# A streaming encoder layer: the gate's norm folded behind its mix, operand splits moved into the passes, and a fourth accumulator copy per pair

## The chip, the cores and the metric

The kernel runs on one NeuronCore of a Trainium2 chip. The metric is device time in microseconds for one execution; before the change three runs took 1078.3, 1076.97 and 1076.26 us, so the median is 1076.97 us. The execution under the profiler took 1074.96 us, with a span of 1073.2 us from its first to its last instruction.

The engines are called by the profile's names: PE is TensorE, which multiplies (PEld is its weight load), DVE is VectorE, ACT is ScalarE, POOL is GpSimd, and SP only issues transfers. Each engine runs its own list of instructions strictly in order, and semaphores are the only link between the lists.

## The reference

One layer is computed for 2048 prompt frames and 8 x 16 sample frames, with d = 1024.

```python
h = x @ w_in                                   # 3 * 512 columns for part A, 4 * 512 for part B
u_a = gelu(h[..., 0:512])
v_a = layernorm(gelu(h[..., 512:1024]), ln_v_g, ln_v_b)
z_a, q, k, v_b, z_b = the five groups of 512 columns that follow
# part A, in chunks of 128 frames, 4 groups g of 128 channels c
mix = einsum('gts,bnsgc->bntgc', tril(w_s), v_a) + b_s      # b_s: one number per g and t
a_out = u_a * mix
# part B: attention over the own 64-frame chunk and the 8 before it, 8 heads, relative bias
b_out = softmax(q k^T / 8 + bias) v_b
y = concat(a_out * silu(z_a), b_out * silu(z_b))
out = layernorm(ALPHA * x + y @ w_out, ln_g, ln_b)
```

The sample frames take the same path with cached keys and values; k, v_b and the normalised v_a of the sample frames are outputs too (`gv_out` holds the last).

## The kernel before

The 2176 frames are 17 token tiles of 128. All matrix products are done on rounded operands (fp32r) in three parts: every operand is split into a high part, which ACT makes by a copy, and a low part, which DVE makes by subtracting the high part from the original. PE then adds high x high, high x low and low x high.

**The va stage** (17 tiles, some 130 us). For tile t PE does `project_tile("va", t, ..)` in two halves h (L1667, 12 products of 512 columns each), and between the halves `mix(t - 2)` (L1683, four plain fp32 products of 128 columns). ACT moves the projection out of PSUM with Gelu (L1131), DVE does the layer norm on it in four instructions (L1412 statistics, L1414 their mean and variance, L1416 subtract and times gain, L1425 times rstd and plus offset), with rstd from POOL (L957, L959). ACT copies the mix out (L1061), POOL adds b_s (L939), and SP stores it to the scratch tensor `s_mix`. Beside that, the tiles' own operands `xt_f`, `xt_h`, `xt_l` are loaded and split two tiles ahead (L1047 on ACT, L1340 on DVE), and the operand of the first pass is prepared.

**The two passes** (some 200 and 227 us) compute everything but va and v_b, for 1024 and 1152 frames. A pass has ten pairs m of 128-column blocks, in the order u, za, u, za, k, k, q, q, z, z. A pair is 2 x 2 blocks, computed with seven products p = 0..6 in place of eight. The seven right operands are combinations of x: `xo_h[a][p]`, `xo_l[a][p]`, each in four pieces kc; POOL forms the combinations (`sum_x`, L905), ACT and DVE split the 28 pieces of a pass (L1054, L1346). The seven left operands `wf` are built one pair ahead (POOL L923 to L929, ACT L1042, DVE L1334). The table `X_IN_TILE` says in which tile, and `X_IN_STEP` in which product of the pass, a piece is split; 24 pieces are split in the va stage and 4 in products 0 to 3 of the first pass, and all 28 of the second pass in the eight v tiles between the passes.

Products accumulate in four PSUM tiles: p = 0, 2, 4 in `sums[0]`, p = 3 in `sums[1]`, p = 1 and 6 in `sums[2]` (the names pt_ps in the profile), p = 5 in `sums[3]`. ACT copies `sums[0]` after p = 0, 2 and 4 (`copy_sum`, L1071). DVE forms the four results ("units") of a pair by one addition each (`add_sums`, L1360), after p = 3, 4, 5 and 6. The second addition reads `sums[2]`, which p = 6 writes on top of, so p = 6 waits for it (`pe.wait_ge(added, 4 * m + 2)`). The first product on `sums[2]` of the next pair (p = 1) waits for all four additions.

A u unit gets Gelu on ACT (L1078) and is multiplied with its part of the mix on POOL (`gate_u`, L949); the part comes back from `s_mix` by a transfer into one of two buffers `mixb`, and the transfer of unit j + 2 waits for gate j. Other units get a Tanh or copy on ACT and one or two operations on DVE (`finish_unit`).

**Token tiles of v_b**: eight between the passes, five behind the second pass, four more beside the first attention steps; the rest of the run (from 667 us) is attention and the output projection. Between the passes the second pass's x is loaded (`load_xo(1, ..)`), summed on POOL (16 instructions) and split. In these stretches tile t + 1's operand shares its memory with the accumulator copies, so SP loads it after the last addition of the pass.

The order of work is written out by hand: each engine's list is what its loops and tables say. What stands behind a waiting instruction waits with it, SP's transfers too.

## Time and profile before

| | PE | DVE | ACT | POOL |
|---|---|---|---|---|
| busy, us (share of the span of 1073.2) | 1010.8 (94%) | 716.9 (67%) | 515.6 (48%) | 324.6 (30%) |
| instructions | 7456 | 1230 | 1018 | 269 |

| | us |
|---|---|
| median of three runs | 1076.97 |
| profiled execution, its own time | 1074.96 |
| its span | 1073.2 |

The profiled execution lies 2.0 us under the median. The busy figure of PE hides three things: matmul records overlap in the pipeline, a product at the half clock counts as busy for twice as long, and 94% is a mean over stages. So the stages are read one by one: the granted clock and the busy time of each stretch, then the gaps of PE on the timeline with the engine that ended each of them, then what that engine's own list did in the gap.

### The profile page before, as it was taken

What the parts mean: (1) busy time and instruction counts of PE and PEld (TensorE: products, weight loads), DVE (VectorE), ACT (ScalarE), POOL (GpSimd) and SP (SyncE); (2) the same over time, 40 slices, a digit from 0 to 9 for tenths busy, and PEclk for the clock granted to TensorE, in tenths of its full rate; (3) what the DMA queues carried; (4) which work ended last, traced back from release to release, by engine and by line L of the source; (5) the groups of instructions that cost most, each with busy time, mean ns of one, the idle gap of its engine ahead of it and who ended that gap; (6) DMA issues with size and microseconds to landing.
All of it is one profiled execution on the core that took longest, in us unless ns stands there. A gap on an engine that the chain in (4) does not pass through costs nothing.

```text
span 1073.2 us, 19266 instructions
## 1 busy us (share of the span) xinstructions
PE 1010.8 (94%) x7456; PEld 865.3 (81%) x7456; DVE 716.9 (67%) x1230; ACT 515.6 (48%) x1018; POOL 324.6 (30%) x269
## 2 busy tenths in 40 slices
PE   7979889999998789999999989999999999999997
PEld 6867677878886569999999977777888888888885
DVE  5959976476565794646555551596777777786765
ACT  5335443334444453333434342575666666666630
POOL 2635753532330834242322200003322222223201
PEclk9998999999999889999999999999999999999999
DMA  6684333346456723323455466575344433433222
GB/s 237 190 232 157 99 108 105 114 121 175 148 145 210 247 94 98 89 92 94 146 175 152 128 200 229 199 261 206 131 149 139 157 133 131 157 121 109 90 80 79
DMA packets 126363, 158.95 MB, mean 148 GB/s; under 512 B 13608, under 2 KB 76224, under 8 KB 126272
## 3 DMA queue, kind: packets, MB, share of 16 engines
q1 hardware_dynamic: 111296, 130.45, 37.8%
q10 hardware_dynamic: 14976, 27.27, 8.0%
q8 instruction: 59, 0.97, 0.4%
q14 instruction: 32, 0.26, 0.1%
HBM read 112.57 MB, written 48.26 MB: 150 GB/s over the span
## 4 chain that ended last, share of the span: by engine, by line
PE 72%; DVE 13%; DMA 6%; issue 3%; ACT 2%; SPq 2%; POOL 1%; ACTq 0%; DVEq 0%
PE s_ps L1713 19%; PE oo_ps L1894 15%; PE pt_ps L1713 9%; PE s_ps L1667 6%; PE oo_ps L1856 6%; PE s_ps L1785 5%; DVE xo_l L1346 4%; PE oo_ps L1713 4%; DMA xt_f<-x_tiles 3%; PE pt_ps L1827 3%; DVE wf L1334 2%; DVE cs L1360 2%; PE s_ps L1894 2%; DVE xt_l L1340 1%; ACT st L1085 1%
## 5 line engine op out<-in xcount | busy, mean ns | idle before, releaser
L1713 PE MATMUL s_ps<-xo_h,wf 128*128 128x288 f32 (+1 forms) x960 | 233.7, 328 | 4.2 <-DVE wf L1334 4.2
L1667 PE MATMUL s_ps<-wp,xt_h 128*128 128x512 f32 x448 | 148.8, 415 | 32.5 <-DVE xt_l L1340 32.0
L1713 PEld LDWEIGHTS s_ps<-xo_h,wf 128*128 128x128 f32 x960 | 164.2, 188 | 17.6 <-DVE xo_l L1346 4.6
L1713 PE MATMUL s_ps<-xo_l,wf 128*128 128x288 f32 (+1 forms) x480 | 157.0, 327 | 0.0
L1667 PEld LDWEIGHTS s_ps<-wp,xt_h 128*128 128x128 f32 x448 | 87.1, 200 | 55.2 <-issue 30.7
L1713 PE MATMUL pt_ps<-xo_h,wf 128*128 128x288 f32 (+1 forms) x480 | 120.8, 329 | 6.8 <-DVE cs L1360 6.6
L1492 DVE CUSTOM_DVE_ANT_1 prob<-s_ps,bias 128x640 f32<-128x640 f32 (+1 forms) x112 | 85.7, 803 | 59.0 <-PE s_ps L1785 59.0
L1228 ACT ACTIVATE prob<-prob,low 128x640 f32<-128x640 f32 (+3 forms) x128 | 97.4, 762 | 45.5 <-DVE low L1492 45.4
L1894 PE MATMUL oo_ps<-wo_h,yh 128*128 128x512 f32 x248 | 100.5, 405 | 0.0
L1334 DVE TENSOR_TENSOR wf<-s,wf 128x512 fp32r<-128x512 f32 x60 | 51.6, 862 | 69.6 <-ACT wf L1042 69.6
L1894 PE MATMUL oo_ps<-wo_h,yl 128*128 128x512 f32 x248 | 97.0, 391 | 0.0
L1894 PE MATMUL oo_ps<-wo_l,yh 128*128 128x512 f32 x248 | 97.0, 391 | 0.0
L1713 PEld LDWEIGHTS pt_ps<-xo_h,wf 128*128 128x128 f32 x480 | 82.3, 188 | 17.2 <-DVE wf L1334 9.0
L1713 PEld LDWEIGHTS s_ps<-xo_l,wf 128*128 128x128 f32 x480 | 90.5, 188 | 6.3
L923 POOL TENSOR_TENSOR s<-a,a 128x512 f32<-128x512 f32 x20 | 26.5, 1323 | 220.3 <-DMA a<-w_pair 220.3
L1667 PE MATMUL s_ps<-wp,xt_l 128*128 128x512 f32 x224 | 91.2, 407 | 0.0
L1334 DVE TENSOR_TENSOR wf<-a,wf 128x512 fp32r<-128x512 f32 x80 | 76.1, 964 | 19.4 <-ACT wf L1042 19.4
L1340 DVE TENSOR_TENSOR xt_l<-xt_f,xt_h 128x512 fp32r<-128x512 f32 x68 | 56.1, 837 | 47.6 <-ACT xt_h L1047 47.6
L1516 DVE TENSOR_SCALAR prob<-prob,rden 128x640 f32<-128x640 f32 (+4 forms) x128 | 79.5, 621 | 4.6
L1713 PE MATMUL pt_ps<-xo_l,wf 128*128 128x288 f32 (+1 forms) x240 | 78.2, 326 | 0.0
L1071 ACT ACTIVATE copy<-s_ps 128x512 f32<-128x512 f32 (+1 forms) x60 | 37.2, 620 | 83.3 <-PE s_ps L1713 83.3
L1002 POOL TENSOR_TENSOR rstd_o<-mv_o,eps 128x1 f32<-128x1 f32 x17 | 3.2, 190 | 235.9 <-DVE mv_o L1567 206.3
(154 smaller groups left out, 2069.1 us busy)
## 6 DMA issues: line engine op xcount, KB each, us to landing
a<-w_pair ACTq DMA_DIRECT2D x80, 256.0 KB, 2.7
...
```

The source lines that it names most:

```text
L1071: nc.scalar.activation(wide(copies[p // 2], pas), sum_at(p, pas), ACT.Copy).then_inc(copied, 1)
L1228: nc.scalar.activation(prob[s][:, 0:n], prob[s][:, 0:n], ACT.Exp, bias=low[:, s:s + 1], scale=-1.0, accum_out=den[:, s:s + 1]).then_inc(ex ...
L1334: nc.vector.tensor_tensor(wf[:, p, 1], operand[p][:], wf[:, p, 0].bitcast(f32), ALU.subtract).then_inc(w_ready, 1)
L1340: nc.vector.tensor_tensor(xt_l[b][h][:], xt_f[b][h][:], xt_h[b][h][:].bitcast(f32), ALU.subtract).then_inc(xt_ready, 1)
L1346: nc.vector.tensor_tensor(xo_l[a][p][:, kc, :], xo_f[a][p][:, kc, :], xo_h[a][p][:, kc, :].bitcast(f32), ALU.subtract).then_inc(xo_ready, 1)
L1492: nc.vector.tensor_tensor_reduce(out=out, in0=src, in1=b, scale=1.0, scalar=MASKED, op0=ALU.add, op1=ALU.min, accum_out=low[:, s:s + 1]).t ...
L1516: nc.vector.tensor_scalar(prob[s][:, lo:n], prob[s][:, lo:n], rden[:, s:s + 1], None, ALU.mult).then_inc(normed, 1)
L1667: made = nc.tensor.matmul(out, xx[b][h][:, kc % HK, :], wp[:, kc, side, :], start=(h, i, a) == (0, 0, 0), stop=(h, i, a) == (1, HK - 1, 2))
L1713: made = nc.tensor.matmul(out, wf[:, p, side, kc, :], xx[pas][p][:, kc, c * n:(c + 1) * n], start=kc == 0 and a == 0 and p in (0, 1, 3, 5) ...
L1785: last = nc.tensor.matmul(s_ps[h][:, at_c:at_c + count * P], q[t % 2][rows, a * GRP + p, :], key_slots(rows, c * GRP + p, first, count), s ...
L1856: last = nc.tensor.matmul(o_ps[64 * h:64 * h + 64, p * P:(p + 1) * P], v[(t + 1 - nk + b) % KR][:, p * P + 64 * h:p * P + 64 * h + 64], pt ...
L1894: last = nc.tensor.matmul(out_bank(half), y[n % 2][:, c, :], w[h][:, c, :], start=c == 0 and a == 0, stop=c == KC - 1 and a == 2)
```

## The change

Three things are changed.

**The norm.** With v = n * g + b, where n is the normalised tile without gain and offset, the mix is W v = g * (W n) + b * rowsum(W). So DVE's two instructions per tile (gain and offset) go; ACT normalises in place by one instruction (`normalise_va`, scale rstd, bias `shift_v` = -mean * rstd, which POOL makes by one more small instruction). PE computes the row sums once, by two fp32 products of 512 columns in front of mix(0), into the PSUM tiles `row_ps`, the first of which is also the output of mix(1). DVE turns them into `mix_b` and `mix_bs` by 4 + 4 instructions of 128 x 128 at the end of its tile 2, and mix(1) waits for the first four. POOL's 17 additions of b_s go, and DVE's eight copies that filled `bss`; gain and offset come back in `scale_mix`, one DVE instruction per u unit (two in the second pass) on the reloaded `mixb`, ahead of that unit's `add_sums`. `gv_out` is made by two DVE instructions in the first pass.

**The splits.** Of the 28 pieces of a pass, the 16 of p = 0..3 are split in the token tiles (tiles 3 to 14 of va; tiles 2, 3, 5, 6 of v), and the 12 of p = 4..6 in products 0 to 3 of the pass, three each. The loads of x move from tiles 0, 2, 5, 8 to 0, 1, 3, 5, and POOL does two sums per tile in tiles 1 to 8. The operand halves have seven places instead of three pairs: half 0 of the second v tile of a stretch goes to the memory of `mixb`, and is loaded in the last pair of the pass; half 1 is loaded one addition earlier and ahead of the last unit's store. The reloads of v tiles 0 and 1 for attention move behind the load of v tile 12.

**The fourth copy.** Ahead of the copy after p = 4, ACT also copies `sums[2]` to `copies[0]`. The second addition then reads two copies, and p = 6 waits for that ACT copy instead of for the addition. In every product the weight builds now stand ahead of `hand` and `finish_unit`.

```diff
-COPY_OF = [0, 2, 2, 1]
+COPY_OF = [0, 0, 2, 1]
...
+X_FIRST = [(kc, p) for kc in range(HK) for p in range(4)]
+X_REST = [(kc, p) for p in range(4, OPS) for kc in range(HK)]
...
-X_IN_TILE[0].setdefault(16, []).extend([(3, 0), (3, 1), (3, 2)])
-for _j in range(28):
-    X_IN_TILE[1].setdefault(min(1 + _j // 4, V_MID - 1), []).append((_j // 7, _j % 7))
-X_IN_STEP = [{0: [(3, 3)], 1: [(3, 4)], 2: [(3, 5)], 3: [(3, 6)]}, {}]
...
+for _j, _piece in enumerate(X_FIRST):
+    X_IN_TILE[0].setdefault(3 + 3 * _j // 4, []).append(_piece)
+    X_IN_TILE[1].setdefault((2, 3, 5, 6)[_j // 4], []).append(_piece)
+X_IN_STEP = {step: X_REST[3 * step:3 * step + 3] for step in range(4)}
...
+    if kind == "v" and h == 0 and t in (1, V_MID + 1):
+        return 6
+    if tile_seq(kind, t) % 2:
+        return 2 + h
+    return 4 + h if kind == "v" and t > V_MID else h
...
-        copies = [at(f"copy{j}", copy_at + 4 * WIDTH[1] * j, [WIDTH[1]]) for j in range(3)]
+        copies = [at(f"copy{j}", copy_at + 4 * WIDTH[1] * i, [WIDTH[1]]) for j, i in enumerate((1, 0, 2))]
...
+        mix_b, mix_bs = at("mix_b", here, [GRP, P]), at("mix_bs", here + 2048, [GRP, P])
...
+        row_ps = [out_ps, pt_both[:, 1].rearrange("p g t -> p (g t)")]
...
-                    if h == 0 and t in (0, 2, 5, 8):
-                        load_xo(0, (0, 2, 5, 8).index(t))
+                    if h == 0 and t in (0, 1, 3, 5):
+                        load_xo(0, (0, 1, 3, 5).index(t))
...
+                            load_xt("v", t + 1, 0)
+                sp.wait_ge(added, 4 * NP * (pas + 1) - 1)
+                load_xt("v", V_MID * pas + 1, 1)
...
-            sp.wait_ge(u_mixed, len(U_UNITS))
...
+                if t == V_MID + 2:
+                    sp.wait_ge(xt_freed, tile_number("v", V_MID + 1))
+                    load_v(0)
+                    load_v(1)
...
-            def add_bias_s(t):
...
-                pool.wait_ge(mixb_loaded[j % 2], 16 * (j // 2 + 1))
+                pool.wait_ge(mix_scaled, j + 1)
...
-                if t >= 1:
-                    sum_x(0, t - 1)
-                if t >= 2:
-                    add_bias_s(t - 2)
+                for j in (2 * t - 2, 2 * t - 1):
+                    if 0 <= j < 16:
+                        sum_x(0, j)
...
+                pool.wait_ge(rstd_v_ready, t + 1)
+                nc.gpsimd.tensor_scalar(shift_v[:], mv_v[:, 0:1], rstd_v[:], -1.0,
+                                        ALU.mult, ALU.mult).then_inc(shift_v_ready, 1)
...
+            def normalise_va(t):
+                act.wait_ge(shift_v_ready, t + 1)
+                nc.scalar.activation(st[t % 2][:, 0:512], st[t % 2][:, 0:512], ACT.Identity, bias=shift_v[:],
+                                     scale=rstd_v[:]).then_inc(vn_ready, 1)
...
+                if p == 4:
+                    act.wait_ge(added, 4 * m + 1)
+                    nc.scalar.activation(wide(copies[0], pas), sum_at(1, pas), ACT.Copy).then_inc(copied, 1)
...
-                    act.wait_ge(added, 4 * m - 3 if p == 0 else 4 * m)
-                pas = m // NP
+                    act.wait_ge(added, 4 * m - 2 if p == 0 else 4 * m)
...
-                dve.wait_ge(copied, 3 * m + (1 if p == 3 else 3))
-                nc.vector.tensor_tensor(wide(unit_sum(n), pas), sum_at(p, pas) if p != 4 else sum_at(1, pas),
+                dve.wait_ge(copied, 4 * m + (1 if p == 3 else 4))
+                nc.vector.tensor_tensor(wide(unit_sum(n), pas), sum_at(p, pas) if p != 4 else wide(copies[2], pas),
...
+            def scale_mix(n):
+                if n not in U_COUNT:
+                    return
+                pas, _, g, tb = unit_of(n)
+                j = U_COUNT[n] - 1
+                dve.wait_ge(mix_b_ready, 2 * GRP)
+                dve.wait_ge(mixb_loaded[j % 2], 16 * (j // 2 + 1))
+                held, add = mixb[j % 2][:, 0:512].rearrange("p (n t) -> p n t", t=P), mix_b[:, g, :]
+                made = nc.vector.scalar_tensor_tensor(out=held, in0=held, scalar=v_cols[:, g:g + 1],
+                                                      in1=bass.AP(add.tensor, add.offset, [add.ap[0], [0, 4], [1, P]]),
+                                                      op0=ALU.mult, op1=ALU.add)
+                if pas:
...
-                nc.vector.scalar_tensor_tensor(out=va, in0=va, scalar=mv_v[:, 0:1], in1=lnvg[:], op0=ALU.subtract,
-                                               op1=ALU.mult).then_inc(vn_centred, 1)
...
-                nc.vector.scalar_tensor_tensor(out=va, in0=va, scalar=rstd_v[:], in1=lnvb[:], op0=ALU.mult,
-                                               op1=ALU.add).then_inc(vn_ready, 1)
...
+                if t == 2:
+                    dve.wait_ge(cols_loaded, 32)
+                    dve.wait_ge(row_sums, 2)
+                    for g in range(GRP):
+                        nc.vector.scalar_tensor_tensor(out=mix_b[:, g, :], in0=row_ps[0][:, g * P:(g + 1) * P],
+                                                       scalar=v_cols[:, GRP + g:GRP + g + 1], in1=bs[:, g, :],
+                                                       op0=ALU.mult, op1=ALU.add).then_inc(mix_b_ready, 1)
...
+                    for what in step_builds(step):
+                        w_low_part(what)
+                    for kc, o in X_IN_STEP.get(step - first, ()):
+                        xo_low_part(pas, kc, o)
                     if p >= 4:
                         finish_unit(4 * m + p - 4)
                     if p == 0 and step > first:
                         finish_unit(4 * m - 1)
-                    for what in step_builds(step):
-                        w_low_part(what)
...
+                    if p >= 3:
+                        scale_mix(4 * m + p - 3)
...
+                    for row, held in zip(row_ps, (wt, wts)):
+                        nc.tensor.matmul(row[:], st[3][:, 0:P], held[:].rearrange("p g t -> p (g t)"),
+                                         start=True, stop=True).then_inc(row_sums, 1)
...
+                if t == 1:
+                    pe.wait_ge(mix_b_ready, GRP)
...
-                    pe.wait_ge(added, 4 * m + 2)
+                    pe.wait_ge(copied, 4 * m + 3)
```

How the lists move, at three places. First DVE in va tile 9, before (xt_l and xo_l are the low parts, st the tile):

```order
L1412 BN_STATS stats_v_148<-st1_115 128x6
L1414 BN_AGGR mv_v_149<-stats_v_148 128x2
L1416 SCALAR_TENSOR_TENSOR st1_115<-st1_115,mv_v_149,lnvg_91 128x512
L1340 TENSOR_TENSOR xt_l1_0_132<-xt_f1_0_138,xt_h1_0_126 128x512
L1346 TENSOR_TENSOR xo_l0_1_64<-xo_f0_1_78,xo_h0_1_50 128x512
L1346 TENSOR_TENSOR xo_l0_2_65<-xo_f0_2_79,xo_h0_2_51 128x512
L1425 SCALAR_TENSOR_TENSOR st1_115<-st1_115,rstd_v_150,lnvb_92 128x512
L1340 TENSOR_TENSOR xt_l1_1_133<-xt_f1_1_139,xt_h1_1_127 128x512
```

and the same tile after:

```order
L1445 BN_STATS stats_v_152<-st1_114 128x6
L1449 BN_AGGR mv_v_153<-stats_v_152 128x2
L1358 TENSOR_TENSOR xt_l2_132<-xt_f2_139,xt_h2_125 128x512
L1364 TENSOR_TENSOR xo_l0_0_63<-xo_f0_0_77,xo_h0_0_49 128x512
L1364 TENSOR_TENSOR xo_l0_1_64<-xo_f0_1_78,xo_h0_1_50 128x512
L1358 TENSOR_TENSOR xt_l3_133<-xt_f3_140,xt_h3_126 128x512
```

The two scaled instructions on st are gone; this tile still has two pieces of xo, others have one.

Second, DVE in va tile 2, before:

```order
L1412 BN_STATS stats_v_148<-st0_114 128x6
L1414 BN_AGGR mv_v_149<-stats_v_148 128x2
L1416 SCALAR_TENSOR_TENSOR st0_114<-st0_114,mv_v_149,lnvg_91 128x512
L1340 TENSOR_TENSOR xt_l0_0_130<-xt_f0_0_136,xt_h0_0_124 128x512
L1425 SCALAR_TENSOR_TENSOR st0_114<-st0_114,rstd_v_150,lnvb_92 128x512
L1340 TENSOR_TENSOR xt_l0_1_131<-xt_f0_1_137,xt_h0_1_125 128x512
```

and after (mix_b is what mix(1) on PE waits for):

```order
L1445 BN_STATS stats_v_152<-st0_113 128x6
L1449 BN_AGGR mv_v_153<-stats_v_152 128x2
L1358 TENSOR_TENSOR xt_l0_130<-xt_f0_137,xt_h0_123 128x512
L1358 TENSOR_TENSOR xt_l1_131<-xt_f1_138,xt_h1_124 128x512
L1460 SCALAR_TENSOR_TENSOR mix_b_146<-oo_ps,v_cols_157,bs_93 128x128 x4
L1465 SCALAR_TENSOR_TENSOR mix_bs_147<-pt_ps,v_cols_157,bs_93 128x128 x4
```

The first four of the new instructions stand behind both halves' splits of tile 4.

Third, DVE from the first addition of pair 0 (u) on, before:

```order
L1360 TENSOR_TENSOR u0_0_110<-s_ps1,copy0_97 128x512
L1334 TENSOR_TENSOR wf_101<-a11_106,wf_101 128x512
L1360 TENSOR_TENSOR u1_1_113<-pt_ps,copy2_99 128x512
L1334 TENSOR_TENSOR wf_101<-s1_100,wf_101 128x512
L1360 TENSOR_TENSOR u1_0_112<-oo_ps,copy2_99 128x512
L1334 TENSOR_TENSOR wf_101<-s2_109,wf_101 128x512
L1360 TENSOR_TENSOR u0_1_111<-pt_ps,copy1_98 128x512
```

and after (mixb is a reloaded part of the mix, cs and u are results, copy the accumulator copies):

```order
L1429 SCALAR_TENSOR_TENSOR mixb0_117<-mixb0_117,v_cols_157,mix_b_146 128x512
L1380 TENSOR_TENSOR u0_0_109<-s_ps1,copy0_96 128x512
L1352 TENSOR_TENSOR wf_100<-a11_105,wf_100 128x512
L1429 SCALAR_TENSOR_TENSOR mixb1_118<-mixb1_118,v_cols_157,mix_b_146 128x512
L1380 TENSOR_TENSOR u1_1_112<-copy2_98,copy0_96 128x512
L1352 TENSOR_TENSOR wf_100<-s1_99,wf_100 128x512
L1429 SCALAR_TENSOR_TENSOR mixb0_117<-mixb0_117,v_cols_157,mix_b_146 128x512
L1380 TENSOR_TENSOR u1_0_111<-oo_ps,copy2_98 128x512
L1352 TENSOR_TENSOR wf_100<-s2_108,wf_100 128x512
L1429 SCALAR_TENSOR_TENSOR mixb1_118<-mixb1_118,v_cols_157,mix_b_146 128x512
L1380 TENSOR_TENSOR u0_1_110<-pt_ps,copy1_97 128x512
```

Each addition to u now stands behind an instruction that needs a transfer into mixb, and the second addition reads two copies.

## Rows read from the trace of the kernel before

**Rows 1.** Stretches: us, busy (instructions) by engine, PEclk, DMA share, GB/s.

```profile
22.63:73.69 51.06, 51.06 (x256) 43.10 (x256) 43.49 (x52) 18.80 (x34) 27.81 (x29) 1.00 0.62 183
73.69:137.98 64.29, 48.14 (x225) 38.97 (x225) 58.36 (x66) 31.48 (x57) 38.97 (x36) 0.92 0.48 149
137.98:337.56 199.58, 196.00 (x856) 159.89 (x857) 125.64 (x160) 81.73 (x145) 71.89 (x49) 0.99 0.47 138
337.56:404.05 66.49, 50.89 (x194) 39.47 (x192) 52.20 (x52) 32.97 (x59) 32.90 (x19) 0.87 0.52 170
404.05:631.08 227.03, 223.85 (x1682) 222.84 (x1682) 124.73 (x153) 87.71 (x160) 65.46 (x45) 1.00 0.42 124
631.08:666.97 35.89, 30.55 (x122) 23.95 (x121) 10.88 (x17) 10.50 (x18) 1.50 (x4) 0.90 0.71 246
```

**Rows 2.** Chain that ended last, in time: start, us, piece, instructions merged.

```profile
241.31 2.72 PE s_ps L1713 x12
...
244.03 2.98 PE pt_ps L1713 x12
...
420.18 3.18 PE oo_ps L1713 x24
```

**Rows 3.** Timeline, PE, 80 to 140: start, us, line, operation, idle before.

```profile
81.53 1.19 PE L1667 MATMUL s_ps<-wp,xt_h 128*128 128x512 f32 x2 [7.84 <-DVE xt_l L1340]
...
121.95 1.16 PE L1683 MATMUL oo_ps<-wt,st 128*128 128x128 f32 x8 [1.29 <-DVE st L1425]
...
129.87 1.16 PE L1683 MATMUL oo_ps<-wt,st 128*128 128x128 f32 x8 [1.28 <-DVE st L1425]
...
137.98 0.76 PE L1713 MATMUL s_ps<-xo_h,wf 128*128 128x512 f32 x1 [4.18 <-DVE wf L1334]
```

**Rows 4.** Timeline, PE, 170 to 180: product 6 of a pair.

```profile
177.72 0.47 PE L1713 MATMUL pt_ps<-xo_h,wf 128*128 128x512 f32 x1 [0.88 <-DVE cs L1360]
```

**Rows 5.** Timeline, PE then POOL, 340 to 400: token tiles between the passes.

```profile
377.87 1.19 PE L1667 MATMUL s_ps<-wp,xt_h 128*128 128x512 f32 x2 [4.09 <-DVE xt_l L1340]
...
351.59 29.24 POOL L905 TENSOR_TENSOR xo_f<-xo_f,xo_f 128x576 f32<-128x576 f32 x16 [34.34 <-DMA xo_f<-x_t]
```

**Rows 6.** Timeline, PE then SP, 630 to 660: token tiles after the second pass.

```profile
640.70 1.19 PE L1667 MATMUL s_ps<-wp,xt_h 128*128 128x512 f32 x2 [3.84 <-DVE xt_l L1340]
...
640.18 4.26 SPq L666 DMA_DIRECT2D v<-v_all  x2
...
646.46 2.83 SPq L595 DMA_DIRECT2D xt_f<-x_tiles  x2
```

**Rows 7.** Timeline, DVE, 120 to 140: a split next to GpSimd's work, and one alone.

```profile
124.65 3.48 DVE L1346 TENSOR_TENSOR xo_l<-xo_f,xo_h 128x512 fp32r<-128x512 f32 x2
...
131.97 0.68 DVE L1346 TENSOR_TENSOR xo_l<-xo_f,xo_h 128x512 fp32r<-128x512 f32 x1
```

**Rows 8.** Timeline, ACT, 20 to 90: splits and copies that waited for DMA.

```profile
33.73 0.63 ACT L1047 ACTIVATE xt_h<-xt_f 128x512 fp32r<-128x512 f32 x1 [3.31 <-DMA xt_f<-x_tiles]
...
77.94 0.60 ACT L1061 ACTIVATE st<-oo_ps 128x512 f32<-128x512 f32 x1 [13.66 <-DMA s_mix<-st]
```

**Rows 9.** Timeline, PE, 20 to 30: one mix in eight records.

```profile
25.48 1.05 PE L1683 MATMUL oo_ps<-wt,st 128*128 128x128 f32 x8
```

**Rows 10.** Groups by line and form: DVE's small gate; the activation table loads.

```profile
L1544 DVE SCALAR_TENSOR_TENSOR ysb<-s_ps,zs 64x64 f32<-64x64 f32 x16 | 3.5, 218 | 0.3
...
L1228 ACT ACT_TABLE_LOAD x1 | 1.3, 1283 | 0.0
```

**Rows 11.** Timeline, POOL, 120 to 140: the power in the norm.

```profile
123.67 0.87 POOL L959 TENSOR_TENSOR rstd_v<-rstd_v,minus_half 128x1 f32<-128x1 f32 x1
```

**Rows 12.** The reloads of mixb: SP's issue, landing times, and DVE's third sum.

```profile
197.30 7.79 SPq L619 DMA_DIRECT2D mixb<-s_mix  x4
...
DMA to landing us min/median/max: 2.6/2.7/3.9
...
199.00 0.68 DVE L1360 TENSOR_TENSOR u<-oo_ps,copy 128x512 f32<-128x512 f32 x1
```

More of the change, by code:

```diff
@@ L649, in mixb_after @@
                     j = U_COUNT[n] - 1
-                    if j + 2 < len(U_UNITS):
+                    if j + 2 < len(U_UNITS) and j + 2 not in (8, 9):
                         sp.wait_ge(u_mixed, j + 1)
@@ L870, in _ @@
                 sp.wait_ge(r_stored[s], 16 * n_stores)
+            sp.wait_ge(gv_stored, 16)
             for s in range(2):
```

200 lines of the change are left out of this document (102 added, 98 removed).

## The prediction

> **What bounds the kernel now.** I read the stretches first, then the gaps of PE on its timeline, then the list of the engine that ended each gap. In the stretches [rows 1] the reader is to see that PE is the bound, but not everywhere. Tiles 2 to 9 of va run without a gap at the full clock (51.06 us for eight tiles, 6.38 each). The next stretch needs 64.29 us for seven tiles, which at 6.38 are 44.7. The passes are nearly tight: a product of the first is 2.72 us and of the second 3.18 [rows 2], so seventy need 190.4 and 222.6, and the stretches are 199.58 (with two mixes, 1.8 by the price below) and 227.03. That leaves 7.4 and 4.4 us. The eight v tiles between the passes take 66.49 us with PE at 0.87 of the clock; at 12 operations of 0.227 (2.72 / 12) per half they need 43.6. The five behind the second pass take 35.89 for 27.2. Losses: 19.6, 7.4, 22.9, 4.4, 8.7, together 63 us.
>
> What ends PE's gaps [rows 3 to 6] is DVE, every time, and DVE is late for three reasons. In va's tiles 12 to 16 it is full: a tile's period is 7.92 us (121.95 to 129.87), with 1.28 lost before each mix. A split takes 0.68 alone and 1.74 beside GpSimd's sums [rows 7]; two engines that read two SBUF operands take turns. Around tile 10 it waited for ACT, which stood 13.66 us before a copy into a slot whose store hung behind the bias table's transfers [rows 8]. In the v tiles it waits for operands that SP loads late, or is full itself.
>
> The Trainium skill ("SBUF — State Buffer", section "Who interferes with whom") says that a DVE operation with two SBUF inputs and a GpSimd operation that reads SBUF exclude each other for a whole instruction. The pair of splits at 3.48 agrees [rows 7]. By that rule the change has a cost that its diff hides: the second addition now has two SBUF inputs instead of one. Twenty additions at up to a split's 1.06 us of waiting would be 21 us of DVE time, but in 3.18 us products only little of it on the path.
>
> **The change, part by part.** Everything is relative to the 1074.96 us of the profiled execution, which is 2.0 under the median of 1076.97.
>
> *va stage, given back.* Two DVE operations per tile go to one on ACT, and the splits fall from two to 1.3 a tile. A tile of DVE was 7.92; it loses 2 x 0.6 for the norm, at least 0.4 for splits, and turns with POOL's addition (1.06): some 5.3, under the 6.38 of PE. So DVE's excess ends. PE's last va tile ends at 133.80 now (137.98 less 4.18), and from 81.53 seven tiles need 44.7, to 126.2: 7.6 lost, of which I take 2.0 as half clock behind the gap at 81.53, an estimate from the stretch's mean clock of 0.92 [rows 1], so 5.6 goes. The 4.18 before the first product [rows 3] goes too: the three splits in front of the five weight builds are gone, and ACT makes those builds' high parts while PE is in the last tile. One DVE operation less ahead of xt_l takes 0.7 off the start and 0.7 off the gap at 81.53. Sum: -11.2.
>
> *va stage, added.* Row sums: a mix of 4 x 128 columns takes 1.05 us as recorded [rows 9], and 0.9 by the period of a tile (6.38 less 24 operations of 0.227); two products of 512 columns are twice that, 1.8, on the path. Then mix(1) waits for mix_b. DVE reaches mix_b only behind the second split of tile 4, whose operand ACT can copy at 33.73 at the earliest today, because its transfer starts when tile 2 has left it [rows 8]. That is 4.7 us after tile 2's end (22.63 + 6.38); the one DVE operation less brings it 0.7 forward, and the copy itself takes 0.63. Adding the split (0.6) and four small operations (between 0.22, the 64 x 64 row of [rows 10], and 0.68, [rows 7]; I take 0.25, since 128 columns are nearest to the small row), mix_b is ready at 6.2 after tile 2, and PE wants it after one half, at 2.7: a wait of 3.5 (2.5 to 5). The half clock that followed the gap at 81.53 could follow it, 0 to 2; I take 1. Sum: +6.3. The stage: -4.9 (-13 to 0).
>
> ACT's new instruction stands behind DVE's statistics and three POOL instructions, the longest 0.87 [rows 11]; the chain ends some 3.8 us after a tile's Gelu starts, inside 6.38, and the mix wants it 9 us after. I cost it at nothing. Whether ACT must load a table between Gelu and Identity, this trace doesn't show: it has three loads in all, of 1.283 us [rows 10]. Bounds 0 and 2 x 1.283 per tile; I take 0, because Copy and Identity stand between the other functions without one. The Trainium skill ("ScalarE: Activation LUTs", section "Table sets: the hidden batching unit") says that identity is in every set, which would make it 0.
>
> *The passes.* p = 6 waited for an addition in every pair: 0.88 us at 177.72 [rows 4], and 0.26 in most (2.98 against 2.72, [rows 2]). The new copy is ready during p = 4. ACT gains 20 copies of 0.6, which its idle 60% hides. With builds ahead of `hand` and `finish_unit`, DVE reaches its additions sooner. I take half of the 7.4 and three quarters of the 4.4: -3.7 and -3.3. Against that: the additions of u units stand behind the reload of mixb. In pair 2 the reload was issued at 197.30 and takes 2.6 to 3.9 [rows 12], so landed at 199.9, where the third addition ran at 199.00. The fourth's comes 3 us later, 202.9; scale and add, 1.4, give 204.4 against 203.2, when PE wants to start p = 1 of the next pair: 1.1 each for pairs 0 and 2, +2.2. The second pass's 0.46 longer products hide it. The 12 splits in products 0 to 3 are 8.2 us of DVE and as much of ACT, under 10.9 of PE; no cost, up to 3 if GpSimd interferes. Sum: -4.8 (-9 to +2).
>
> *v tiles between the passes.* The operand of tile 1 no longer comes late, and 12 of 28 splits leave DVE, which ends the stretch's gaps. They are at least 12 x 0.69 = 8.3 us of it. Its partner does 16 sums in 29.24 us, and sets a floor [rows 5]: 351.6 + 29.2, three more sums, and the last eight splits give a first product near 395, for 404.05. I take -8.5. Bounds: -14 (GpSimd's 16 sums a sixth shorter, since fewer turns are taken) and -3 (the same gaps, 4.09 and its like, one tile later).
>
> *v tiles behind the second pass.* The gap of 3.84 at 640.70, and the half clock after it, come from tile 9's late load; its first half is now there. Tile 11's load was issued at 646.46, behind the reloads of v that held SP for 4.26 us [rows 6]; these move behind it. Of 8.7 lost I leave 2.4, for a queue that is full of q, k and bias: -6.3 (-8 to -2). From there on nothing changes but the date.
>
> Sum: -4.9 - 4.8 - 8.5 - 6.3 = -24.5, so 1050.5 us; I say 1050.
>
> **Rivals.** *A, more of it goes (chance 0.19).* mix_b comes within the half, the clock stays up, and the middle tiles go down to the transfers: -10, -7, -13, -8 gives -38, 1037. For it: DVE has slack wherever it is not full. Against: the load that mix_b stands behind can't start earlier. *B, DVE stays the bound (0.20).* Sharing with GpSimd stretches scale, additions and splits, and the middle tiles keep their gaps: -2, -2, -4, -5 gives -13, 1062. For it: 3.48 for two splits. Against: GpSimd loses 17 additions of b_s. *C, slower (0.04).* One mechanism: in the four u pairs DVE's whole list stands behind the mixb reload, the gate on GpSimd behind DVE, and the next reload behind the gate. A round is 2.6 to 3.9 of transfer, 0.7 to 1.7 of scale, 1.3 to 1.7 of gate. Each u pair has two such waits, and builds for the next pair stand behind them. It decides from 27 / 4 = 6.8 us a pair, where I have 1.1 in two of them; at 8 a pair the time is 1080. *D, the mixes and the copy do nothing for the path (0.03):* PE's gaps only move from DVE to ACT, whose list now holds norm, splits and copies; within 2 us of 1075.
>
> **How the numbers follow.** The forecast, 1043 to 1056, has 0.54. The range of 8 in 10 takes in A's 1037 and B's 1062: 1037 to 1063. A measurement of this kernel can tell 0.2%, 2 us, from no change. Faster by more: forecast, A and B and a little of D, 0.94; slower 0.04; within it 0.02.
>
> **What would show it.** The profile after should have the first product of pass 0 at 132 to 134, with a gap of PE of about 3.5 us in tile 3 ended by DVE's mix_b and no gap before mixes 13 and 14; the gap near tile 10 still there, 7 us. In the passes no PE gap in front of p = 6, and gaps of about 1 us before p = 1 of pairs 1 and 3 of the first pass alone. Between the passes some 58 us, still with DVE-ended gaps; behind them 29 to 30 us. Three table loads. I am wrong if the va stretch ends later than 138, if there are more than three table loads, or if gaps in the u pairs exceed 3 us.

## The result: slower, where a gain of 2.5% was forecast

The changed kernel took 1081.03 us (median of 7 runs, 1078.73 to 1082.59), the kernel before 1078.2 us beside it: a ratio of 1.0032 (95% interval 1.0019 to 1.0045), 0.3% slower, or 3.4 us. The forecast was 1050 us, its range 1037 to 1063. The profiled execution took 1081.03 us (span 1079.3), 6.07 more than that of before; the stages below are read from these two executions, so they add up to 6 and not to 3.4. All ratios, and the medians of the table of experiments, leave out two executions at a much lower granted clock (1633.81 us at 0.558 of before_fourth_copy, and 1357.58 us at 0.749 of the kernel before).

The same six stretches [rows 1] after (us, then busy PE, PEld, DVE, ACT, POOL, then PEclk, DMA share, GB/s):

```profile
21.48:73.77 52.29, 46.46 (x216) 38.40 (x217) 27.83 (x45) 23.91 (x41) 29.47 (x36) 0.93 0.50 155
73.77:137.23 63.46, 56.19 (x271) 47.14 (x270) 24.59 (x43) 31.07 (x54) 19.60 (x31) 0.92 0.58 171
137.23:343.30 206.07, 195.46 (x858) 160.11 (x856) 147.00 (x176) 92.75 (x168) 68.81 (x48) 0.99 0.46 132
343.30:403.75 60.45, 47.71 (x193) 37.68 (x192) 46.94 (x42) 27.06 (x47) 32.49 (x19) 0.94 0.58 198
403.75:634.88 231.13, 225.10 (x1681) 224.28 (x1680) 150.15 (x180) 98.92 (x181) 68.19 (x45) 0.99 0.42 122
634.88:670.69 35.81, 29.94 (x122) 23.67 (x120) 9.75 (x15) 10.21 (x17) 1.51 (x4) 0.90 0.72 241
```

| stage | before | after | difference | forecast |
|---|---|---|---|---|
| start to product 0 | 137.98 | 137.23 | -0.75 | -4.9 |
| first pass | 199.58 | 206.07 | +6.5 | -4.8 with the second |
| second pass | 227.03 | 231.13 | +4.1 | in the line above |
| v tiles between | 66.49 | 60.45 | -6.0 | -8.5 |
| v tiles behind | 35.89 | 35.81 | -0.1 | -6.3 |
| attention, output | 406.23 | 408.61 | +2.4 | 0 |

The passes are half of the 30.6 us by which the forecast missed (+10.6 for -4.8). The last line was forecast at 0, and took 403.8 to 408.6 in the profiled executions of all kernels here: its 2.4 can't be told from scatter. Where PE stood (timeline of PE, [idle before, what ended it]):

```profile
38.43 2.05 PE L1738 MATMUL oo_ps<-wt,st 128*128 128x128 f32 x8 [5.83 <-DVE mix_b L1460]
...
90.37 1.19 PE L1717 MATMUL s_ps<-wp,xt_h 128*128 128x512 f32 x2 [7.27 <-DVE xt_l L1358]
...
165.81 0.47 PE L1770 MATMUL pt_ps<-xo_h,wf 128*128 128x512 f32 x1 [3.72 <-DVE u L1380]
...
188.46 0.47 PE L1770 MATMUL pt_ps<-xo_h,wf 128*128 128x512 f32 x1 [1.74 <-DVE cs L1380]
...
209.82 0.47 PE L1770 MATMUL pt_ps<-xo_h,wf 128*128 128x512 f32 x1 [2.04 <-DVE u L1380]
...
432.99 0.37 PE L1770 MATMUL pt_ps<-xo_h,wf 128*128 128x288 f32 x1 [3.65 <-DVE u L1380]
...
481.65 0.37 PE L1770 MATMUL pt_ps<-xo_h,wf 128*128 128x288 f32 x1 [2.00 <-DVE u L1380]
...
657.55 1.19 PE L1717 MATMUL s_ps<-wp,xt_h 128*128 128x512 f32 x2 [5.79 <-DVE xt_l L1358]
```

Of [rows 3] the gaps before the mixes and the 4.18 before product 0 are gone, and the gap of 7.84 is 7.27; new is 5.83 at mix(1). Of [rows 4] the wait of p = 6 is gone, and a longer one stands before p = 1 (165.81 and the next four rows; 230.90 has another, of 1.76). What DVE did before the first of them (timeline), and two pieces of the chain of waits there (start, us, what):

```profile
152.19 1.78 DVE L1429 SCALAR_TENSOR_TENSOR mixb<-mixb,v_cols,mix_b 128x512 f32<-128x512 f32 x1
...
155.61 1.78 DVE L1429 SCALAR_TENSOR_TENSOR mixb<-mixb,v_cols,mix_b 128x512 f32<-128x512 f32 x1
...
157.31 1.77 DVE L1380 TENSOR_TENSOR u<-copy,copy 128x512 f32<-128x512 f32 x1
...
159.73 0.75 DVE L1429 SCALAR_TENSOR_TENSOR mixb<-mixb,v_cols,mix_b 128x512 f32<-128x512 f32 x1
...
164.29 0.77 DVE L1429 SCALAR_TENSOR_TENSOR mixb<-mixb,v_cols,mix_b 128x512 f32<-128x512 f32 x1 [2.12 <-DMA mixb<-s_mix]
...
164.99 0.68 DVE L1380 TENSOR_TENSOR u<-pt_ps,copy 128x512 f32<-128x512 f32 x1
```

```profile
159.93 1.71 POOL u L959
...
161.65 2.55 DMA mixb<-s_mix
```

The reader is to see three things. The second addition has two copies as inputs and takes 1.77 us, where one with a PSUM input takes 0.68 (164.99). The scaling ahead of it, which also reads two tiles in SBUF, takes 1.78; the next one, at 159.73, takes 0.75, and when it starts POOL has no instruction running (none from 158.54 to 159.89). And the fourth addition stands behind a scaling that waited 2.12 us for its reload: POOL began the gate that frees the buffer at 159.93, as soon as the second addition had gone through ACT's Gelu, the transfer followed it at 161.65, and PE started p = 1 at 165.81, right behind the addition.

### The profile page after: what moved, and what is told of

The parts are those of the page before. It is cut to its first block, busy times and chain, and to the rows that moved or that the text cites. A ratio compares the mean times of both kernels' runs of the same rounds, so it can differ in the third digit from the quotient of the medians.

```text
span 1079.3 us, 19336 instructions
## 1 busy us (share of the span) xinstructions
PE 1012.7 (94%) x7460; PEld 869.6 (81%) x7460; DVE 706.6 (65%) x1222; ACT 535.6 (50%) x1055; POOL 305.5 (28%) x269
## 4 chain that ended last, share of the span: by engine, by line
PE 73%; DVE 9%; DMA 7%; issue 4%; ACT 3%; POOL 2%; SPq 2%; DVEq 0%; ACTq 0%; POOLq 0%
PE oo_ps L1951 16%; PE s_ps L1770 15%; PE pt_ps L1770 9%; PE s_ps L1717 8%; PE oo_ps L1913 6%; PE s_ps L1842 5%; DMA xt_f<-x_tiles 4%; PE oo_ps L1770 3%; PE pt_ps L1884 3%; PE pt_ps L1717 2%; DVE xo_l L1364 2%; PE s_ps L1951 2%; DVE cs L1380 1%; PE s_ps L1871 1%; PE oo_ps L1738 1%
## 5 line engine op out<-in xcount | busy, mean ns | idle before, releaser
L1717 PE MATMUL s_ps<-wp,xt_h 128*128 128x512 f32 x448 | 146.4, 409 | 29.7 <-DVE xt_l L1358 27.5
L1358 DVE TENSOR_TENSOR xt_l<-xt_f,xt_h 128x512 fp32r<-128x512 f32 x68 | 63.6, 945 | 84.4 <-ACT xt_h L1057 84.2
L1352 DVE TENSOR_TENSOR wf<-s,wf 128x512 fp32r<-128x512 f32 x60 | 54.0, 902 | 74.3 <-ACT wf L1052 74.3
L1352 DVE TENSOR_TENSOR wf<-a,wf 128x512 fp32r<-128x512 f32 x80 | 61.1, 783 | 21.9 <-ACT wf L1052 21.9
L1842 PE MATMUL s_ps<-k,q 64*128 64x256 f32 (+3 forms) x696 | 67.5, 322 | 3.6 <-DVE low L1542 3.5
```

The costliest lines, as they stand in the source:

```text
L1352: nc.vector.tensor_tensor(wf[:, p, 1], operand[p][:], wf[:, p, 0].bitcast(f32), ALU.subtract).then_inc(w_ready, 1)
L1358: nc.vector.tensor_tensor(xt_l[b][:], xt_f[b][:], xt_h[b][:].bitcast(f32), ALU.subtract).then_inc(xt_ready, 1)
L1717: made = nc.tensor.matmul(out, xx[b][:, kc % HK, :], wp[:, kc, side, :], start=(h, i, a) == (0, 0, 0), stop=(h, i, a) == (1, HK - 1, 2))
L1842: last = nc.tensor.matmul(s_ps[h][:, at_c:at_c + count * P], q[t % 2][rows, a * GRP + p, :], key_slots(rows, c * GRP + p, first, count), s ...
```

## The experiments

All ratios are to the kernel before on the same chip, 5 rounds; 0.01 is 10.8 us.

| kernel | median us | ratio (95%) | first, second pass us |
|---|---|---|---|
| changed | 1081.03 | 1.0032 (1.0019-1.0045) | 206.07, 231.13 |
| scale_behind_add | 1066.07 | 0.9894 (0.9882-0.9907) | 201.35, 223.58 |
| mix_b_in_tile_1 | 1072.24 | 0.9950 (0.9936-0.9963) | 206.68, 232.55 |
| before_fourth_copy | 1088.09 | 1.0098 (1.0078-1.0118) | 208.65, 228.12 |
| after_three_copies | 1067.53 | 0.9913 (0.9900-0.9925) | 201.47, 226.42 |
| after_add_from_psum | 1070.02 | 0.9944 (0.9924-0.9964) | 200.72, 229.31 |
| before_fourth_from_psum | 1078.01 | 1.0011 (0.9990-1.0031) | 199.91, 229.68 |
| three_mends | 1053.85 | 0.9786 (0.9764-0.9808) | 198.13, 222.59 |
| three_mends_skew_later | 1044.12 | 0.9704 (0.9680-0.9728) | 197.82, 222.59 |
| after_old_order | 1105.56 | 1.0255 (1.0234-1.0275) | 222.69, 241.78 |
| before_new_order | 1070.43 | 0.9933 (0.9915-0.9951) | 196.20, 222.68 |
| mends_three_copies | 1045.31 | 0.9695 (0.9671-0.9720) | 198.01, 222.59 |
| mends_bias_later | 1039.45 | 0.9645 (0.9624-0.9666) | 198.48, 222.60 |
| before_order_skew_later | 1060.62 | 0.9833 (0.9807-0.9859) | 197.84, 222.70 |
| before_order_fourth | 1072.36 | 0.9942 (0.9921-0.9962) | 197.84, 223.61 |

**The reload in front of the addition.**

```diff
-                    if p >= 3:
-                        scale_mix(4 * m + p - 3)
                     ...
                     add_sums(m, p)
+                    if p >= 3:
+                        scale_mix(4 * m + p - 3)
```

> The changed kernel (1081.0 us) with one edit: in a step of the passes DVE makes the addition of a unit first and scales the reloaded mixb behind it, so that no addition stands behind a reload. Theory 1 (reload loop): the gaps of PE before p = 1 that end with an addition to u (3.72 and 2.04 us in the first pass, 3.65 and 2.00 in the second) come from the reload alone; they go, with some 3 us of half clock behind the two long ones: 1067 us (1064 to 1070). Theory 2 (DVE has too much work, or waits for GpSimd on two-input operations): the same instructions are still on DVE, each u pair keeps a gap of 2 us or more: 1076 us or above.

-14.9 us by the ratios, and 1066.07 us: theory 1's time. Of its account only part came true. The gaps of 3.65 and 2.00 us in the second pass are gone, but in the first pass that of 3.72 is now 1.77 and that of 2.04 is 1.12:

```profile
163.53 0.47 PE L1770 MATMUL pt_ps<-xo_h,wf 128*128 128x512 f32 x1 [1.77 <-DVE u L1380]
...
184.53 0.47 PE L1770 MATMUL pt_ps<-xo_h,wf 128*128 128x512 f32 x1 [1.71 <-DVE cs L1380]
...
204.97 0.47 PE L1770 MATMUL pt_ps<-xo_h,wf 128*128 128x512 f32 x1 [1.12 <-DVE u L1380]
```

What is left in the u pairs, and all of the za pairs' gap (184.53), is not the reload.

**mix_b earlier.** The two loops that make `mix_b` and `mix_bs` move from `if t == 2` to `if t == 1`.

> The changed kernel (1081.0 us) with one edit: DVE makes mix_b and mix_bs at the end of its va tile 1 instead of tile 2. Theory 1: mix(1) then waits under 1 us instead of 5.83, and the half clock behind it (2.8 us) goes: 1072.5 us (1071 to 1075), and everything behind tile 3 starts 8 to 9 us earlier. Theory 2: a transfer sets the stage, not mix_b, so the time comes back in the gap of 7.27 us near tile 10: 1080 us.

Theory 1: -8.8 us by the ratios, and no gap at mix(1). The gap near tile 10 did not take it back:

```profile
83.42 1.19 PE L1717 MATMUL s_ps<-wp,xt_h 128*128 128x512 f32 x2 [6.78 <-DVE xt_l L1358]
```

Why mix_b was later than forecast is seen in tile 2 of the changed kernel, ACT then DVE:

```profile
34.17 0.81 ACT L1075 ACTIVATE st<-st,shift_v,rstd_v 128x512 f32<-128x512 f32 x1 [3.13 <-POOL shift_v L972]
...
34.89 0.61 ACT L1057 ACTIVATE xt_h<-xt_f 128x512 fp32r<-128x512 f32 x1
```

```profile
35.53 1.71 DVE L1358 TENSOR_TENSOR xt_l<-xt_f,xt_h 128x512 fp32r<-128x512 f32 x1 [2.44 <-ACT xt_h L1057]
...
37.17 1.12 DVE L1460 SCALAR_TENSOR_TENSOR mix_b<-oo_ps,v_cols,bs 128x128 f32<-128x128 f32 x4
```

The copy that the split needs stands on ACT behind the new normalising instruction, which waited 3.13 us for POOL; the split, beside POOL's sums, took 1.71.

**The fourth copy.** On the kernel before, alone:

```diff
-COPY_OF = [0, 2, 2, 1]
+COPY_OF = [0, 0, 2, 1]
...
+                if p == 4:
+                    act.wait_ge(added, 4 * m + 1)
+                    nc.scalar.activation(wide(copies[0], pas), sum_at(1, pas), ACT.Copy).then_inc(copied, 1)
...
-                    pe.wait_ge(added, 4 * m + 2)
+                    pe.wait_ge(copied, 4 * m + 3)
```

> The kernel before (1078.2 us) with the fourth copy alone: ACT copies sums[2] ahead of the copy after p = 4, the second addition reads two copies, p = 6 waits for that copy. Norm, splits, loads and the place of the builds stay. Theory 1: the gaps before p = 6 (0.26 us in most pairs, 0.82 to 1.04 in the two za pairs of each pass) go and nothing takes their place: 8 us less at most, 1071 to 1074 us. Theory 2: in the za pairs the gap only moves to p = 1 of the next pair, since DVE's finishing work is what is late, and only the 0.26 of the others is gained: 1075 us. Theory 3: the addition with two SBUF inputs waits for GpSimd (1.77 us instead of 0.68 in the changed kernel) and this eats the gain: 1078 us.

None of the three: 11 us slower than the kernel before (1.0098). Undone in the changed kernel:

> The changed kernel (1081.0 us) without the fourth copy: the second addition reads sums[2] again and p = 6 waits for it. Theory 1: the copy is worth its 0.26 us per pair and a za pair's 0.9: 1084 to 1087 us; in the u pairs p = 6 now also stands behind a mixb that is scaled ahead of the second addition. Theory 2: the passes are bound by DVE's order and not by p = 6: within 1 us of 1081.

Neither here: 12.8 us faster, where theory 1 had it slower and theory 2 unchanged, and within some two microseconds of what moving the scaling gave.

First, what was there to gain. Both expectations, like the prediction, take the 0.26 us of most pairs for a wait of p = 6. The chain of the kernel before shows that it is not. The two pieces ahead of those in [rows 2] are these:

```profile
235.87 2.72 PE oo_ps L1713 x12
...
238.59 2.72 PE pt_ps L1713 x12
```

The order is p = 5 (oo_ps), p = 6 (pt_ps, 2.72 us: no wait), p = 0 of the next pair (s_ps at 241.31) and p = 1 (pt_ps at 244.03). The piece of 2.98 us is p = 1, which waits for the fourth addition. In the kernel before, p = 6 waited in the za pairs alone: 0.88 and 0.82 us in the first pass, 1.04 and 0.91 in the second, 3.65 us in all.

Second, what it cost. DVE's four additions of a pair are one chain: addition, ACT's Tanh or copy of it, finishing work on DVE, build, next addition. PE starts p = 1 of the next pair no earlier than the chain ends, and it has four products to do in that time (p = 4, 5, 6 and 0). Here is the same za pair, first in the kernel before:

```profile
171.50 0.69 DVE L1360 TENSOR_TENSOR cs<-s_ps,copy 128x512 f32<-128x512 f32 x1 [0.94 <-PE s_ps L1713]
...
176.89 0.68 DVE L1360 TENSOR_TENSOR cs<-pt_ps,copy 128x512 f32<-128x512 f32 x1
...
183.53 0.68 DVE L1360 TENSOR_TENSOR cs<-pt_ps,copy 128x512 f32<-128x512 f32 x1
```

and in before_fourth_copy (DVE, then the instruction on POOL beside the second addition, then the gap of PE behind the chain, then two groups of additions by tile: duration ns min/median/max):

```profile
175.37 0.69 DVE L1363 TENSOR_TENSOR cs<-s_ps,copy 128x512 f32<-128x512 f32 x1 [0.93 <-PE s_ps L1716]
...
180.77 1.77 DVE L1363 TENSOR_TENSOR cs<-copy,copy 128x512 f32<-128x512 f32 x1
...
183.24 0.69 DVE L1377 SCALAR_TENSOR_TENSOR st<-st,cs 128x512 f32<-128x512 f32 x1 [0.70 <-ACT st L1088]
...
188.50 0.68 DVE L1363 TENSOR_TENSOR cs<-pt_ps,copy 128x512 f32<-128x512 f32 x1
```

```profile
180.47 1.53 POOL L929 TENSOR_TENSOR s<-a,s 128x512 f32<-128x512 f32 x1 [0.17 <-POOL a L927]
```

```profile
189.33 0.47 PE L1716 MATMUL pt_ps<-xo_h,wf 128*128 128x512 f32 x1 [3.17 <-DVE cs L1363]
```

```profile
L1363 DVE TENSOR_TENSOR cs<-copy,copy x16: 693/1774/1846, 180.8 to 639.6; 128x512 f32<-128x512 f32 x8, 128x576 f32<-128x576 f32 x8
...
L1363 DVE TENSOR_TENSOR cs<-pt_ps,copy x16: 684/717/758, 188.5 to 645.8; 128x512 f32<-128x512 f32 x8, 128x576 f32<-128x576 f32 x8
```

The addition from two copies has a median of 1.77 us, that from PSUM 0.72. In this pair the chain took 12.7 us before (171.50 to 184.21) and takes 13.8 now (175.37 to 189.18), where four products are 10.9: the 1.1 us lands on it whole. The 0.88 us that p = 6 no longer waits only brings PE to p = 1 earlier, and the gap there is 3.17 us where it was 0.92. In a k pair (242.37 to 253.34) the chain is 11.0 us against 10.7 before, and its gap of some 0.3 us stays. So the chain, not p = 6, is the second bound of the passes, and the u and za pairs pay most for the copy: all four in the first pass have gaps of 1.15 to 3.17 us before p = 1 now. The Trainium skill ("SBUF — State Buffer", section "Who interferes with whom") has the rule that a DVE instruction with two SBUF inputs contends with a GpSimd instruction that reads SBUF; these rows agree. So the cure should be one input from PSUM:

```diff
-  sum_at(p, pas) if p != 4 else wide(copies[2], pas),
+  sum_at(p, pas),
...
                 if p == 0 and m:
                     pe.wait_ge(copied, 4 * m)
+                    pe.wait_ge(added, 4 * m - 2)
```

> The changed kernel (1081.0 us) with one edit: the second addition reads sums[0] from PSUM, where product 4 left it, and copies[0], so it has one SBUF input instead of two; the first product on sums[0] of the next pair (and of the next v tile) waits for it. p = 6 is as free as in the changed kernel. Theory 1 (two SBUF inputs wait for GpSimd): the addition goes from 1.8 us in u pairs and 1.5 to 1.8 in the others to 0.72, the chain of four additions gets 1.05 us shorter, and with it each gap before p = 1 (3.72, 1.74, 2.04, 1.76 in the first pass, 3.65 and 2.00 in the second): 1075 us (1073 to 1077). Theory 2: the length of that addition is hidden, and the gaps come from the reload of mixb alone: 1081 us. Theory 3: sums[0], held longer, makes p = 0 of the next pair wait: above 1081.

> The kernel before with the fourth copy (1089.1 us), and the same edit: the second addition reads sums[0] and copies[0]. Theory 1: the 11.6 us that the fourth copy cost came from the addition's second SBUF input, through a chain of addition, ACT's copy, finishing work, build and next addition that is over 10.9 us (four products) long: the gaps before p = 1 (10.8 us in the first pass, 4.4 in the second) shrink by 1.05 each, to some 4.5 and 1.4: 1078 us (1076 to 1081), no better than before. Theory 2: the added ACT copy or its wait is what costs, whatever the addition reads: 1087 us or above.

The first is -9.5 us by the ratios, more than the 6 of theory 1, whose mechanism it bears out. The six gaps are 0.55 to 1.13 shorter, together 5.2, and the two passes of the profiled execution 7.2; the other 2.3 lie within the intervals of the two ratios. The second is theory 1, at the kernel before's own time (1.0011, 0.9990 to 1.0031): made cheap, the copy buys nothing there.

**The order of the builds.** In the changed kernel, put back; and in the kernel before, changed alone (on DVE; on ACT the same with `hand`):

```diff
-                    if p >= 4:
-                        finish_unit(4 * m + p - 4)
-                    if p == 0 and step > first:
-                        finish_unit(4 * m - 1)
                     for what in step_builds(step):
                         w_low_part(what)
                     ...
+                    if p >= 4:
+                        finish_unit(4 * m + p - 4)
+                    if p == 0 and step > first:
+                        finish_unit(4 * m - 1)
```

> The changed kernel (1081.0 us) with the builds of a step back behind hand (on ACT) and finish_unit (on DVE), as in the kernel before. Theory 1 (chain of additions): between two additions DVE idles 0.70 us for ACT's Tanh or copy and then still has the build to do; with the build ahead, it fills that wait. Undone, the chain is up to 3 x 0.70 us longer in every pair that finishes a unit, and the gaps of 0.28 us before p = 1 that the kernel before has with the fourth copy come back in the k, q and z pairs: 1087 us (1084 to 1091). Theory 2: the order is hidden, since the second addition and the reload set the gaps: 1081 us.

> The kernel before (1077.2 us) with the builds of a step ahead of hand and finish_unit, and nothing else. Theory 1: the chain of additions is up to 2 us shorter per pair; the gaps of the za pairs go (0.88, 0.92, 0.82, 0.96 in the first pass, 1.04, 0.54, 0.91, 0.54 in the second), the 0.26 before p = 6 stay, since the second addition can't be earlier than product 4 and ACT's copy: 1071 us (1069 to 1073). Theory 2: the high part of the build on ACT now stands ahead of hand and of the copies of the accumulator, and this takes the gain: 1077 us.

The second is theory 1's time (-7.2 us), and the order is the best of the parts of the change that were measured alone. Its account has the two kinds of gap the wrong way round. The 0.26 us, which was to stay, went, since it was p = 1 waiting for the end of the chain, and the chain is shorter now (chain that ended last; the second line stands for the 2.98 in [rows 2]). What stayed in the first pass is 0.60 and 0.61 us before p = 6 of the za pairs.

```profile
242.53 2.72 PE s_ps L1713 x12
...
245.25 2.72 PE pt_ps L1713 x12
```

The first is +24 us by the ratios, four times the 6 that theory 1 had. Its gaps, and DVE in the u pair that ends with the first of them:

```profile
168.74 0.77 PE L1770 MATMUL pt_ps<-xo_h,wf 128*128 128x512 f32 x1 [6.38 <-DVE u L1380]
...
193.42 0.47 PE L1770 MATMUL pt_ps<-xo_h,wf 128*128 128x512 f32 x1 [3.17 <-DVE cs L1380]
...
219.37 0.76 PE L1770 MATMUL pt_ps<-xo_h,wf 128*128 128x512 f32 x1 [5.02 <-DVE u L1380]
```

```profile
156.07 1.43 DVE L1352 TENSOR_TENSOR wf<-a,wf 128x512 fp32r<-128x512 f32 x1 [1.22 <-ACT wf L1052]
...
162.37 1.74 DVE L1429 SCALAR_TENSOR_TENSOR mixb<-mixb,v_cols,mix_b 128x512 f32<-128x512 f32 x1
...
167.25 0.74 DVE L1429 SCALAR_TENSOR_TENSOR mixb<-mixb,v_cols,mix_b 128x512 f32<-128x512 f32 x1
```

The gaps of 0.28 us in the k, q and z pairs came back as theory 1 has them; the rest is in the u and za pairs. In a u pair DVE waits 1.22 us, not 0.70, between two additions: ACT makes the Gelu of the unit and only then the high part of the build that DVE wants. Each link of the chain is then that wait, the build, the scaling and the addition, and the scaling at 162.37 takes 1.74, where its like took 0.75 (159.73) in the changed kernel. The reload is no longer waited for at all (no idle time before 167.25). Last, the fourth copy on the new order:

> The kernel before with the new order of the builds (1070.4 us) and the fourth copy as the change has it. Theory 1 (chain against four products): with the build in ACT's wait the chain has some 2 us to spare in most pairs and takes the addition's 1.05 us without a gap; only the za pairs (gap 0.60) get 1.05 longer gaps, four times at most, and p = 6 gains 0.26 in the others: 1071 to 1074 us. The 13.5 us that the same copy costs in the changed kernel are then the copy together with the scaling in the u pairs. Theory 2: the copy costs its 12 us whatever stands around it: 1082 us.

Theory 1: +1 us, which the intervals don't tell from nothing, and gaps of 1.70 and 1.60 us behind the za pairs of the first pass, where 0.60 and 1.05 were to add up. The cost of the copy depends on what slack the chain has: 11 us in the old order, 1 in the new, 13 with the scaling in front.

**Together.**

> The changed kernel with three edits together: scaling behind the addition, mix_b in tile 1, second addition from PSUM. If the three causes are separate, their gains add: 15.0 + 8.8, and for the addition what is left of the gaps before p = 1 (1.77, 1.71, 1.12, 1.67) less 1.05 each, 4 us: 1053 us (1051 to 1056). If mix_b's gain is partly given back near tile 10 or in the token tiles between the passes: 1058 us.

> As three_mends, and the eight transfers of the bias table to s_skew are no longer issued in one row in va tile 7: one goes out in each of the pairs 2 to 9 of the first pass, at p = 3. Theory 1: the gap of 7 us near tile 10 and the half clock behind it (2.5 us) go: 1044 us (1042 to 1048). Theory 2: the transfers now delay the weight pieces that ACT asks for in the passes, or DMA still sets the pace of the va stage: 1050 us or above.

The diff of the second, beside the loop taken out of va tile 7:

```diff
+                        if pas == 0 and m >= 2 and p == 3:
+                            h = m - 2
+                            sp.dma_start(s_skew[h, :, 0:REL], s_rel[h, :].partition_broadcast(P)).then_inc(rel_stored, 16)
```

Both by theory 1 (1053.85 and 1044.12). The second pass is then as tight as 70 products of 3.18, 222.6:

```profile
387.50:610.09 222.59, 222.59 (x1681) 222.59 (x1680) 142.82 (x180) 100.02 (x181) 69.74 (x45) 1.00 0.43 127
```

> As three_mends_skew_later (1044.1 us), but with three copies instead of the fourth one and the addition from PSUM: the second addition reads sums[2] and p = 6 waits for it. Theory 1: a cheap fourth copy is worth what p = 6 waited for, 0.26 us in a pair of the first pass and some more in the u pairs: 1047 us (1046 to 1049). Theory 2: the mends of order have taken over its whole gain: 1044 us.

The two ran on different chips, so the ratios decide: 0.9695 against 0.9704, which puts the kernel with three copies 1 us ahead, within intervals of 2.6 us each. The passes take 198.01 and 222.59 us against 197.82 and 222.59. No gain of the cheap fourth copy is shown, which speaks for theory 2.

> The kernel before with the new order of the builds (1070.4 us) and the transfers of the bias table moved into the first pass, as in the three mends. With the norm on DVE and the splits in the va stage as before. Theory 1: the gap of 8.0 us near tile 9 and the half clock behind it (2.5 us) go: 1060 us; against it, mends_three_copies (1045.3), which differs from this kernel by the folded norm and the moved splits and loads alone, prices these two at 15 us. Theory 2: DVE, full in the last five va tiles, had caught up in that gap, and the gaps before the mixes grow: 1065 us, and the two are worth 20.

-10.8 us, theory 1. Against mends_three_copies the folded norm, the moved splits and the loads are worth 14.9 us (0.9833 less 0.9695), with mix_b in tile 1 and the scaling behind the addition. By the stages of the two profiled executions 7.6 of it lies before product 0 (129.12 for 121.56), 8.0 between the passes (67.77 for 59.74), and nothing in the passes. The norm and the splits were not measured apart.

**Behind the second pass.**

```diff
             load_qk(0)
-            load_qk(1)
-            sp.wait_ge(rel_stored, 16 * (2 + HEADS))
-            ...
-            sp.dma_start(bias[:, 2 * NEAR:].rearrange("p (h j) -> p h j", h=HEADS), near).then_inc(bias_loaded, 16)
             for t in range(V_MID, V_EARLY):
                 ...
+                if t == V_MID + 1:
+                    load_qk(1)
+                    ...
+                    sp.dma_start(bias[:, 2 * NEAR:].rearrange("p (h j) -> p h j", h=HEADS), near).then_inc(bias_loaded, 16)
```

> As three_mends_skew_later (1044.1 us), and behind the second pass SP issues the load of q and k of tile 1 (1 MB) and of the bias (1.28 MB) behind x for v tile 11 instead of ahead of it. Theory 1: that stretch (35.6 us for five tiles that need 27.2) is bound by the bytes in the queue ahead of x: its gap of 6.2 us and the half clock behind it go, 6 to 8 us: 1037.5 us (1036 to 1040). Theory 2: the first attention steps now wait for the bias, which takes 11.5 us to land: 1043 us or above.

-6.4 us by the ratios, 1039.45, the fastest kernel here: 3.5% under the kernel before. In three_mends_skew_later the stretch was 35.63 us with a gap of 6.22 before tile 11. Now it is 32.43, and tile 11 doesn't wait. What is left is a gap before tile 12, whose x is issued behind the bias now:

```profile
625.02 0.81 PE L1721 MATMUL s_ps<-wp,xt_h 128*128 128x512 f32 x2 [3.10 <-DVE xt_l L1360]
```

So theory 1 holds for tile 11, and half of the wait came back one tile later. The stretch gives 3.2 of the 6.4 us; the rest lies within the intervals. In the changed kernel the bias took 11.5 us to land; x for tile 11 was issued behind it, at 647.68, and ACT waited for it until 656.05:

```profile
bias<-s_skew SPq DMA_DIRECT2D x1, 1280.0 KB, 11.5
```

```profile
647.68 0.95 SPq L610 DMA_DIRECT2D xt_f<-x_tiles  x2
```

```profile
656.05 1.34 ACT L1057 ACTIVATE xt_h<-xt_f 128x512 fp32r<-128x512 f32 x2 [9.09 <-DMA xt_f<-x_tiles]
```

## Why the prediction was wrong, step by step

- *va stage, given back (-11.2).* Right: DVE's excess and the 4.18 went, and the stage's -0.75 less what was added (10.4, next) is -11.2. *Added (+6.3)*: the mechanism was right, the size not. "a wait of 3.5 (2.5 to 5)" was 5.83, and the half clock behind it cost 2.8, not 1 (the mix 2.05 for 1.05, a half tile 4.51 for 2.72); with the 1.8 for the row sums, which the step had and no run measures alone, this is 10.4. The step took the transfer for the last thing to arrive. It was ACT's copy, behind the normalising instruction that the step had put down at nothing, and the split behind it took 1.71 us, not 0.6. mix_b_in_tile_1 gives 8.8 for the wait and the clock. About 4 of the 30.6 us.
- *The passes (-4.8, was +10.6): the failed step.* It had three things wrong.
  - The reading of [rows 2]: "p = 6 waited for an addition in every pair". It waited in the za pairs alone, 3.65 us in both passes; the 0.26 us is p = 1, and waits for the chain.
  - The price of the copy: "I take half of the 7.4 and three quarters of the 4.4". That is 7.0 us for the copy and the order of the builds together. The order alone gives 7.2, and the copy alone costs 11. The price of its second SBUF input, 1.06 us, was at hand and was set aside as "only little of it on the path": the step held it against the length of a product, and not against the chain of four additions that p = 1 waits for.
  - The reload: "1.1 each for pairs 0 and 2", and nothing in the second pass. The u pairs' gaps were 3.72 and 2.04, and 3.65 and 2.00 in the second pass. The step timed the reload by when SP issued it before (197.30, [rows 12]). But SP issues it behind a gate, the gate stands behind an addition, and that was now later by the scaling (1.78) and the longer addition.
- *Rival C* (chance 0.04) had this loop and named 1080 us, which is nearly the time measured. That is in part luck: its 1080 needs 8 us a pair from the loop alone, and taking the reload out of the way gave 14.9 us, 3.7 a pair. Reload, scaling and longer addition did it together, and other stages missed their gains too. Its sign, gaps of over 3 us in the u pairs, did come.
- *The 12 splits in products 0 to 3* were put at no cost. In every kernel here that has them, PE has a gap of some 0.85 us before p = 2 of the first pair, ended by ACT's copy (144.59 in the changed kernel).
- *Between the passes (-8.5, was -6.0).* Within its bounds. Gaps of 2.68, 5.23 and 2.71 ended by DVE remain. No experiment took them up.
- *Behind (-6.3, was -0.1).* "these move behind it" took SP for the bound. Tile 9 no longer waited, and the wait came back at tile 11, behind q, k and bias. What is queued ahead of x was the bound: with the second q and k and the bias issued later, tile 11 didn't wait, and tile 12 did for 3.10 us.
- *The table loads* stayed three; the gap at tile 10 was forecast at 7 and was 7.27.
